# Low half of the gate's split weights: an accumulating transfer onto a negated rounded copy, in place of a vector subtraction

## What is computed

```
x += 0.5 * (silu(h @ w_gate) * (h @ w_up)) @ w_down      h = rms_norm(x), w_gate, w_up: 1024 x 2816
```

## Time and profile before

| | |
|---|---|
| median of three runs | 2062.52 us |
| the profiled execution's own time | 2060.64 us |
| its span | 2058.8 us |
| granted TensorE clock, mean | 1.0 (of 2.4 GHz) |
| instructions | 34279 |
| TensorE busy | 99% of the span |
| VectorE, ScalarE, GpSimd busy | 72%, 39%, 27% |
| bytes moved by DMA | 165.22 MB, mean 80 GB/s |

### The profile page before, as it was taken

How to read it: one execution, slowest core, us unless ns; L and a number is a source line. 1 busy time by engine, 2 the same in 40 slices (tenths; PEclk the granted TensorE clock), 3 DMA queues, 4 the chain that set the end, 5 groups by cost and what they waited for, 6 DMA issues and landing times. The chain is left out here.

```text
span 2058.8 us, 34279 instructions
## 1 busy us (share of the span) xinstructions
PE 2039.2 (99%) x13866; PEld 2004.4 (97%) x13866; DVE 1476.8 (72%) x2292; ACT 809.5 (39%) x1342; POOL 547.3 (27%) x382
## 2 busy tenths in 40 slices
PE   8999999999999999999999999999999999999998
PEld 6999999999889999999999999999999999999998
DVE  6896684974665579758487789576677888576685
ACT  5343342442433434334244344243335534333343
POOL 4243232402000025323240134232320045232230
PEclk9999999999999999999999999999999999999999
DMA  5233232333221223323223323323243123323222
GB/s 155 64 86 92 73 98 67 83 100 91 57 60 44 72 62 86 84 77 102 68 81 84 88 57 82 103 62 88 77 118 85 43 66 83 88 77 93 72 57 82
DMA packets 312004, 165.22 MB, mean 80 GB/s; under 512 B 15339, under 2 KB 309431, under 8 KB 311848
## 3 DMA queue, kind: packets, MB, share of 16 engines
q1 hardware_dynamic: 309152, 158.36, 27.8%
q0 software_dynamic: 2576, 4.64, 1.0%
q10 hardware_dynamic: 120, 0.04, 0.0%
HBM read 159.01 MB, written 4.00 MB: 79 GB/s over the span
## 5 line engine op out<-in xcount | busy, mean ns | idle before, releaser
L498 PE MATMUL psum<-xg_hi,in_hi 128*128 128x320 f32 x1952 | 611.3, 313 | 2.9 <-DVE in_lo L1212 2.4
L500 PE MATMUL psum<-xg_hi,in_lo 128*128 128x320 f32 x1952 | 604.5, 310 | 0.0
L499 PE MATMUL psum<-xg_lo,in_hi 128*128 128x320 f32 x1952 | 604.3, 310 | 0.0
L498 PE MATMUL psum<-f_hi,f_out_hi 128*128 128x320 f32 x1408 | 436.6, 310 | 2.1 <-DVE f_out_lo L1220 1.7
L500 PE MATMUL psum<-f_hi,f_out_lo 128*128 128x320 f32 x1408 | 435.1, 309 | 0.0
L499 PE MATMUL psum<-f_lo,f_out_hi 128*128 128x320 f32 x1408 | 435.1, 309 | 0.0
L498 PEld LDWEIGHTS psum<-xg_hi,in_hi 128*128 128x128 f32 x1952 | 367.4, 188 | 9.1 <-issue 3.3
L499 PEld LDWEIGHTS psum<-xg_lo,in_hi 128*128 128x128 f32 x1952 | 367.7, 188 | 0.6
L500 PEld LDWEIGHTS psum<-xg_hi,in_lo 128*128 128x128 f32 x1952 | 367.5, 188 | 0.0
L1662 POOL TENSOR_TENSOR sums<-in_raw 128x512 f32<-128x512 f32 x72 | 100.7, 1399 | 735.0 <-DVE in_lo L1224 474.5
L1224 DVE TENSOR_TENSOR in_lo<-in_raw,in_hi 128x1024 fp32r<-128x1024 f32 x144 | 233.0, 1618 | 55.8 <-ACT in_hi L893 55.8
(11 more groups left out here) (201 smaller groups left out, 2857.2 us busy)
## 6 DMA issues: line engine op xcount, KB each, us to landing
in_raw<-in_ffn_w_gate SPq DMA_DIRECT2D x88, 512.0 KB, 3.9
in_raw<-in_ffn_w_up SPq DMA_DIRECT2D x88, 512.0 KB, 5.2
out_raw<-in_ffn_w_down SPq DMA_DIRECT2D x96, 384.0 KB, 3.3
out_raw<-in_ffn_w_down SPq DMA_DIRECT2D x32, 256.0 KB, 3.0
in_raw<-in_mix_w_in SPq DMA_DIRECT2D x14, 512.0 KB, 4.5
out<-y_nat SPq DMA_DIRECT2D x5, 512.0 KB, 3.2
x_nat<-in_x_prompt SPq DMA_DIRECT2D x4, 512.0 KB, 5.8
in_raw<-in_mix_w_in SPq DMA_DIRECT2D x8, 256.0 KB, 4.6
```

Source lines behind the costliest of these rows:

```text
L498: pe.matmul(dst, w_hi, v_hi, start=first, stop=False)
L499: pe.matmul(dst, w_hi, v_lo, start=False, stop=False)
L500: return pe.matmul(dst, w_lo, v_hi, start=False, stop=last)
```

## The change

The low parts of blocks 0 and 1 (the raw gate weights of a fast chunk, 128 x 1024 float32) are no longer a VectorE subtraction. ScalarE first writes the negated rounded copy into `in_lo` (one more ACTIVATE of 128x1024 in `weights_early`, ahead of the one that writes the high part), counted by `gate_negated`. GpSimd, after the four sums of the chunk, waits for it and issues a DMA from `in_raw` that adds the raw weights onto `in_lo`, counted by `gate_low_landed`. TensorE waits ahead of product 1 for the high part and for the landed transfer. `fast_split` now counts 3 steps a chunk, and the waits on it are renumbered. SyncE waits for the transfer too, before it refills a slot.

```diff
--- before.py
+++ after.py
@@ -287,6 +287,8 @@
 
         sum_done, fast_hi, fast_split = sem("sum_done"), sem("fast_hi"), sem("fast_split")
         prod_mm, p1_done, evac_done, gate_done = sem("prod_mm"), sem("p1_done"), sem("evac_done"), sem("gate_done")
+
+        gate_negated, gate_low_landed = sem("gate_negated"), sem("gate_low_landed")
         block_made, block_hi, block_lo = sem("block_made"), sem("block_hi"), sem("block_lo")
 
         band_mm, band_hi, band_lo = sem("band_mm"), sem("band_hi"), sem("band_lo")
@@ -359,7 +361,8 @@
             phase = [name for name, first in IN_CHUNK.items() if first <= old][-1]
             f = old - IN_CHUNK[phase]
             if phase in FFN_INDEX and f >= PLAIN:
-                eng.wait_ge(fast_split, 4 * fast_chunk(FFN_INDEX[phase], f) + 4)
+                eng.wait_ge(fast_split, 3 * fast_chunk(FFN_INDEX[phase], f) + 3)
+                eng.wait_ge(gate_low_landed, 16 * fast_chunk(FFN_INDEX[phase], f) + 16)
             else:
                 eng.wait_ge(in_split, 2 * (SPLIT_CHUNK[phase] + f) + 2)
 
@@ -597,8 +600,11 @@
 
 
                 for p, (b, bank) in enumerate(zip(PRODUCTS, PRODUCT_BANK)):
-                    if p in (0, 2, 4, 6):
-                        pe.wait_ge(fast_split, 4 * s + p // 2 + 1)
+                    if p == 0:
+                        pe.wait_ge(fast_hi, 4 * s + 1)
+                        pe.wait_ge(gate_low_landed, 16 * s + 16)
+                    elif p in (2, 4, 6):
+                        pe.wait_ge(fast_split, 3 * s + p // 2)
                     if fresh is not None:
                         pe.wait_ge(block_lo, 7 * fresh + BLOCKS.index(b) + 1)
                     if p == 0:
@@ -921,6 +927,7 @@
                     act.wait_ge(in_landed[n % 2], landed(n))
                     if not first:
                         act.wait_ge(prod_mm, 7 * s - 5)
+                    act.activation(weight_slots(in_lo, 0, 2), raw_blocks(n % 2, 0, 2), ACT.Copy, scale=-1.0).then_inc(gate_negated, 1)
                     fast_hi_split((0, 2), raw_blocks(n % 2, 0, 2))
                 if 1 in parts:
                     if not first:
@@ -1363,8 +1370,7 @@
 
                 def weights_early(f):
                     s, n = fast_chunk(index, f), IN_CHUNK[phase] + f
-                    return [(4 * s + 1, (0, 2), raw_blocks(n % 2, 0, 2)), (4 * s + 2, (2, 4), sums[:, 0:2]),
-                            (4 * s + 3, (4, 6), raw_blocks(n % 2, 2, 4))]
+                    return [(4 * s + 2, (2, 4), sums[:, 0:2]), (4 * s + 3, (4, 6), raw_blocks(n % 2, 2, 4))]
 
                 def weights_late(f):
                     fast_lo_split(4 * fast_chunk(index, f) + 4, (6, 7), sums[:, 2:3])
@@ -1380,10 +1386,9 @@
                     elif (i, q) == (2, 1):
                         block_split(index, "B22")
                     elif (i, q) == (2, 3):
-                        for split in weights_early(PLAIN)[0:2]:
-                            fast_lo_split(*split)
+                        fast_lo_split(*weights_early(PLAIN)[0])
                     elif (i, q) == (3, 1):
-                        fast_lo_split(*weights_early(PLAIN)[2])
+                        fast_lo_split(*weights_early(PLAIN)[1])
                     elif (i, q) == (3, 3):
                         weights_late(PLAIN)
 
@@ -1401,9 +1406,9 @@
                             hidden_split(i - 1, 1, u, 0)
                         wait(dve, hidden_done, u - 1)
                         gate_low(s)
-                        ups_begun(s, early[0:1])
-                        ups(s, u, early[1:2])
-                        for split in early[2:3]:
+                        ups_begun(s, [])
+                        ups(s, u, early[0:1])
+                        for split in early[1:2]:
                             fast_lo_split(*split)
                     if g:
                         hidden_split(i, 0, u + 1, 1)
@@ -1658,15 +1663,17 @@
                         pool.wait_ge(block_lo, 7 * index + BLOCKS.index("B21") + 1)
                     elif f in FIRST_CHUNKS:
                         pool.wait_ge(hidden_lo, 44 * index + 2 * f)
-                    wait(pool, fast_split, 4 * s - 2)
+                    wait(pool, fast_split, 3 * s - 2)
                     pool.tensor_tensor(sums[:, 1], raw[:, 0], raw[:, 2], ALU.subtract).then_inc(sum_done, 1)
                     pool.wait_ge(sum_done, 4 * s + 1)
                     pool.tensor_tensor(raw[:, 2], raw[:, 2], raw[:, 3], ALU.add).then_inc(sum_done, 1)
                     pool.wait_ge(sum_done, 4 * s + 2)
                     pool.tensor_tensor(sums[:, 0], raw[:, 2], raw[:, 0], ALU.subtract).then_inc(sum_done, 1)
                     pool.wait_ge(sum_done, 4 * s + 3)
-                    wait(pool, fast_split, 4 * s)
+                    wait(pool, fast_split, 3 * s)
                     pool.tensor_tensor(sums[:, 2], raw[:, 1], sums[:, 0], ALU.subtract).then_inc(sum_done, 1)
+                    pool.wait_ge(gate_negated, s + 1)
+                    pool.dma_start(in_lo[:, 0, 0].bitcast(F32), in_raw[:, n % 2, 0], accum_op=ALU.add).then_inc(gate_low_landed, 16)
 
             pool.memset(ident[:], 0.0).then_inc(ident_cleared, 1)
             pool.wait_ge(ident_cleared, 1)
```

## The result

The changed kernel takes 2116.28 us (median of 4 runs, 2113.0 to 2117.65) against 2062.45 us before: ratio 1.026, 95% interval 1.0244 to 1.0275, 54 us slower. The forecast was 2100 us, 37 us slower, in a range of 2060 to 2182.

A forecast was written before the change was run, and what follows sets the result against it. TensorE's matmul stream, busy 99%, was taken as the bound, so only new waits count. Parts 1 to 4 gave 0 us, the transfer's stalls 35 + 2 = 37 us: 2097.6 us on the profiled run, 2100 us median, range 2060 to 2182.

The forecast's parts named there:

- Parts 1 to 4: VectorE's relief, ScalarE's 72 extra ACTIVATEs, GpSimd's wait and DMA issue, SyncE's later slot refill: each claimed to cost 0 us.
- Part 4: SyncE's slot refill also waits for the transfer; weight loads go out as before, T+5.4 and T+5.8: 0 us by itself.
- Part 5, the issue: Mid-group, the negated copy ends and the transfer is issued, which must land by T+12.32: 4.65 us allowed.
- T+7.65: T is the start of a fast chunk on TensorE; 7.65 us later the negated copy was to end.
- self-mending: A TensorE stall lets the next chunk's negated copy start earlier against T, down to T+4.7, so stalls partly shrink.
- the price of 6.0 us: Transfer from issue to landing: 4.6 us from the h_hist row, 1.2 for the second read, 0.2 for meeting the loads.
- the rival of the hidden transfer: The transfer takes 4.65 us or less, so TensorE doesn't stall and the time stays 2062.5 us; chance 0.28.
- The stall per chunk: TensorE waiting at a fast chunk's start: 0.68 us in 52 chunks and 0.4 us in 4, sum 37 us.
- S = (L - 4.65)/2: Stall S per mid-group chunk from transfer time L, halved by earlier issue after a stall; for S under 1.9 us.
- Slow addition: Rival: adding or descriptor writing is slow, L midway at 8.3 us, costing 119 us, 2182 us in all; chance 0.23.
- Faster: Rival: VectorE's relief removes 1.7 us of TensorE's waits for w_down low parts, 0.1%; chance 0.02 of over 0.2%.
- the forecast case: Moderate TensorE stall, the transfer taking about 4.8 to 7.5 us; chance 0.47, forecast at 2100 us.

The follow-up runs named there:

- experiment 1: The changed kernel without its 72 transfers and the waits for them, ScalarE's negated copies kept: 2060.94 us, ratio 0.9995 to the kernel before.
- experiment 6: Control: the kernel before the change, with only the weight loads issued one step earlier: 2060.74 us, ratio 0.9997.
- experiment 8: The changed kernel with only block 0 by transfer, block 1 subtracted by VectorE again, and weight loads one step earlier: 2062.33 us, ratio 1.0005 to the kernel before.
- experiment 4: The changed kernel with the negated copy ahead of a chunk's first Silu and the transfer issued ahead of GpSimd's last sum: 2115.78 us, ratio 1.0247 to the kernel before.
- experiment 3: The changed kernel with SyncE's weight loads issued one step earlier, about 2.5 us sooner: 2084.57 us, ratio 1.0111 to the kernel before.
- experiment 5: The changed kernel with both weight loads one step earlier and the transfer issued earlier: 2066.33 us, ratio 1.0025 to the kernel before.

## Why the prediction was right, and where it was off

**What bounds the kernel.** Right: relief of VectorE is worth nothing (experiment 1), and the change could only make TensorE wait. Of the signs that were named, the group of VectorE's subtractions fell by 90 us (233.0 to 143.0), though VectorE's busy time as a whole by 77 and not by 89 or more; TensorE's late starts were 38, not 50 or more.

**Parts 1 to 4 at 0 us.** Right for parts 1 to 3, by experiment 1: ScalarE's 72 ACTIVATEs took 1043 ns each, and VectorE's rhythm is TensorE's again. Part 4 was priced at nothing "by itself", and that stands (experiment 6), but it held the larger half of the cause.

**Part 5, the issue.** Predicted at T+7.65, found at T+7.9, and the limit of landing at T+12.3 found as computed; experiment 8 shows that a landing under it costs nothing. T+7.9 holds where the chunk before didn't stall; behind a stall the issue mostly comes at T+6.1 to T+7.7, by the self-mending that the prediction describes.

**Part 5, the price of 6.0 us.** The total was near (median 5.5, mean 5.7 us), but by luck: its parts were wrong and made up for each other. Alone the transfer takes 4.5 us, not 5.8. The nearest row, h_hist, wasn't alone: a transfer of 1152 KB was issued 0.55 us behind it on the same queue, which moved 0.86 MB in those 4.6 us, and I put the second read on top. The loads cost 0.9 us in the changed kernel, not 0.2, and 2.0 us where they are met wholly (experiment 4): I took an overlap of 1.4 us for a small tax, and in fact hardly any of the transfer moves before the loads are through. And instruction fetches, about 1 us each, were in no term, although the profile before lists their queue. The sum that I dismissed was the better one for the transfer alone: 2.2 us for a small transfer on GpSimd's queue, 1.0 us for the bytes and 1.2 us for the second read, 4.4 us, which stood under the rival of the hidden transfer. That rival failed by the two neighbours on the DMA engines: with the loads moved 32 of the 54 us are gone (experiment 3), and with the issue earlier as well, which leaves room for most fetches, 49 (experiment 5).

The Trainium skill (DMA: Bandwidth & Descriptors, Anatomy of one DMA) has 2.0 us + bytes / 436 GB/s, and (Collectives: The Full Stack, on why ReduceScatter is half of AllGather) half the rate for an addition, as it reads two sources. Together that gives estimates of 3.2 and 4.4 us for 256 and 512 KB; measured alone were 3.3 and 4.5 us, and 218 GB/s between the two. The runs agree with both rules. The plain copy alone, at 2.9 us, is a little under the page's 3.2 us.

**The stall per chunk.** Predicted 0.68 us in 52 chunks and 0.4 us in 4, 37 us; found 46 us in 38 chunks. The formula S = (L - 4.65)/2 treats the landings as equal. They aren't, and the gain of a stall goes only to the next chunk: after the stall of 1.55 us the next issue came at T+6.3 (401.66 against 395.33) and its landing, 5.4 us, was 0.6 us too early, which nobody can use. So stalls come in turns, and long landings are paid in full. This is the term of the sum that was mis-sized, 37 us forecast against 46 found; the 8 us of lower clock, 6 of them behind stalls, were missing altogether.

**The rivals.** Slow addition: no, 1.6 us over a copy. Faster: no. Both had been given less than the forecast case, and the sign given 0.70 was the right one.

## What to carry to other kernels

A transfer that takes over an engine's work must be priced by its landing beside everything else on the DMA engines in that stretch, and code fetches belong to that; where it overlaps a bigger load, issuing it earlier gained nothing here until the load was moved. When one engine bounds a kernel without a stall, work taken off another one has no value, and the number to compute is the slack of what replaces it. If the transfer is wanted here all the same, the loads go one step earlier and the issue ahead of the Silu and the last sum.

## What was not expected of the hardware

- With a packet of an instruction queue beside it, an adding transfer of 512 KB lands in 5.6 us in place of 4.5 us (medians of 14 and 48): a single engine ends late.
- A transfer of 512 KB beside a load of 1 MB lands in 6.5 us when issued 1.4 us behind it, and 5.4 us when issued 2.5 us behind it: either way 2.3 us after the load has landed, since its data moves when the load's has.
- After four of the six stalls over 2 us (2.2 to 4.3 us) TensorE's granted clock fell to 1.2 GHz for a little over 3 us; after the other two, 2.3 and 2.4 us long, it did not, and once it fell without a stall before it. What tells these apart is left open.
